# Extra matmuls of ten shapes ahead of 40 feed-forward outputs in each of two networks

## The reference, cut to what matters

```
first:  h = rms_norm(x);  u = conv3(h @ w_up);  gate, val = split(u)
        f = (gelu(gate) * val) @ w_down;  x = x + rms_norm(f)
second: hn = rms_norm(h);  out = h + (silu(hn @ w_gate) * (hn @ w_up)) @ w_down
```

## Time and profile before

| | |
|---|---|
| median of 2 runs | 870.45 us (870.25 to 870.66) |
| profiled execution | 873.64 us, of which 871.9 us from first to last instruction |
| granted TensorE clock, mean | 0.994 of 2.4 GHz |
| PE busy, PEld busy | 95%, 91% of the span |
| DVE, ACT, POOL busy | 73%, 57%, 36% |
| chain that ended last | PE 78%, DVE 10%, ACT 6%, issue 4% |
| DMA | 136 MB, engines busy 49% |

### The profile page before, as it was taken

How to read it: one execution, slowest core, us unless ns; L and a number is a source line. 1 busy time by engine, 2 the same in 40 slices (tenths; PEclk the granted TensorE clock), 3 DMA queues, 4 the chain that set the end, 5 groups by cost and what they waited for, 6 DMA issues and landing times.

```text
span 871.9 us, 16984 instructions
## 1 busy us (share of the span) xinstructions
PE 826.1 (95%) x6722; PEld 789.6 (91%) x6722; DVE 638.7 (73%) x981; ACT 498.8 (57%) x914; POOL 317.6 (36%) x148
## 2 busy tenths in 40 slices
PE   4999999999999999999999789899999999999998
PEld 3998889899999999788999779788999999999998
DVE  6895764888887772768799889955665676667774
ACT  6665655854665657756766474367546544444441
POOL 3843213122333225344466534332454223322321
PEclk9999999999999999999999999999999999999999
DMA  5743234355766665352656542322464457666651
GB/s 209 269 157 107 73 98 145 99 181 152 242 222 188 199 192 170 111 172 98 202 171 192 178 137 74 96 73 77 142 190 149 146 171 230 183 193 191 194 170 49
DMA packets 57246, 137.18 MB, mean 157 GB/s; under 512 B 6352, under 2 KB 27088, under 8 KB 57168
## 3 DMA queue, kind: packets, MB, share of 16 engines
q1 hardware_dynamic: 57168, 136.11, 49.4%
HBM read 135.03 MB, written 1.05 MB: 156 GB/s over the span
## 4 chain that ended last, share of the span: by engine, by line
PE 78%; DVE 10%; ACT 6%; issue 4%; DMA 1%; SPq 0%; DVEq 0%; ACTq 0%
PE PROD L626 15%; PE PROD L627 15%; PE PROD L628 15%; PE PROD L688 3%; PE OP L626 2%; PE OP L627 2%; PE OP L628 2%; PE SC L627 2%; PE TP L627 2%; PE TP L628 2%; PE SC L628 2%; PE TP L626 2%; PE SC L626 2%; DVE RS L1644 2%; PE OP L828 2%
## 5 line engine op out<-in xcount | busy, mean ns | idle before, releaser
L609 POOL TENSOR_TENSOR wlo<-raw,whi 128x1024 fp32r<-128x1024 f32 x124 | 314.0, 2538 | 533.8 <-ACT whi L1118 509.0
L626 PE MATMUL PROD<-HA,whi 128*128 128x256 f32 x1088 | 308.0, 283 | 13.1 <-DVE HA L1665 6.4
L627 PE MATMUL PROD<-HA,wlo 128*128 128x256 f32 x1088 | 302.9, 278 | 0.0
L628 PE MATMUL PROD<-HA,whi 128*128 128x256 f32 x1088 | 302.7, 278 | 0.0
L1118 ACT ACTIVATE whi<-raw 128x1024 fp32r<-128x1024 f32 x252 | 262.7, 1055 | 57.7 <-PE PROD L628 31.5
L1636 DVE TENSOR_TENSOR wlo<-raw,whi 128x1024 fp32r<-128x1024 f32 x128 | 191.0, 1495 | 82.4 <-ACT whi L1118 82.2
L626 PEld LDWEIGHTS PROD<-HA,whi 128*128 128x128 f32 x1088 | 205.9, 189 | 16.5 <-DVE HA L1665 7.0
L627 PEld LDWEIGHTS PROD<-HA,wlo 128*128 128x128 f32 x1088 | 205.3, 189 | 0.8 <-issue 0.7
L628 PEld LDWEIGHTS PROD<-HA,whi 128*128 128x128 f32 x1088 | 205.2, 189 | 0.0
L1644 DVE RECIPROCAL RS<-RTT 128x256 f32<-128x256 f32 (+2 forms) x18 | 42.8, 2380 | 16.6 <-ACT RTT L1137 16.5
L626 PE MATMUL OP<-HA,whi 128*128 128x256 f32 x192 | 53.7, 280 | 0.7 <-DVE KS L1721 0.5
(11 more groups left out here) (330 smaller groups left out, 1622.0 us busy)
## 6 DMA issues: line engine op xcount, KB each, us to landing
raw<-stream SPq DMA_DIRECT2D x197, 512.0 KB, 4.1
raw<-stream SPq DMA_DIRECT2D x144, 128.0 KB, 2.6
raw<-stream SPq DMA_DIRECT2D x28, 256.0 KB, 3.0
raw<-stream SPq DMA_DIRECT2D x4, 384.0 KB, 3.2
X<-xT SPq DMA_DIRECT2D x2, 512.0 KB, 5.5
out<-X SPq DMA_DIRECT2D x8, 128.0 KB, 2.0
KMEM<-memT SPq DMA_DIRECT2D x1, 512.0 KB, 5.4
VMEM<-memT SPq DMA_DIRECT2D x1, 512.0 KB, 6.1
```

The lines of the kernel that those rows point to most:

```text
L609: nc.gpsimd.tensor_tensor(wlo[:, n % NSPLIT, :], raw[:, n % NRAW, :], whi[:, n % NSPLIT, :].bitcast(F32), ALU.subtract).then_inc(lo_pool, 1)
L626: nc.tensor.matmul(dst, wh, hi, start=start, stop=False, skip_group_check=True)
L627: nc.tensor.matmul(dst, wl, hi, start=False, stop=False, skip_group_check=True)
L628: last = nc.tensor.matmul(dst, wh, lo, start=False, stop=stop, skip_group_check=True)
```

## The change

A list of ten shapes (stationary columns, moving columns, how often) is added, and `fm` uses it for the outputs 3 to 42 of "up" and "up2". Ahead of the 24 matmuls of such an output come one or more extra ones. They load the first `columns` columns of the output's first high block and stream the first `width` columns of the first chunk of `HA`'s high part past them, into the bank of the output. Each starts and ends its sum by itself, and the next one, and at last the output's own first matmul, overwrites it: no result of theirs is used. Each entry of the list serves four outputs in a row; the second of the four takes 128 by 128, once, in its place. The entry (P, P, 2) does two. The wait for the tile's low part is placed ahead of the extras as well as ahead of the first block.

```diff
+UNEVEN = [(P, 64, 1), (P, 192, 1), (P, 32, 1), (P, 224, 1), (64, S, 1), (P, 160, 1), (P, 96, 1), (P, P, 2),
+          (32, P, 1), (64, P, 1)]
 ...
                 k = KC[stage]
                 dst = begin((stage, m))[:, 0:S]
+                if stage in ("up", "up2") and 3 <= m < 3 + 4 * len(UNEVEN):
+                    n, i = divmod(POS[FIRST[stage] + m * k], BPT)
+                    if i == 0:
+                        split_wait(pe, n)
+                    columns, width, times = UNEVEN[(m - 3) // 4] if (m - 3) % 4 != 1 else (P, P, 1)
+                    for _ in range(times):
+                        nc.tensor.matmul(dst[0:columns, 0:width], whi[:, n % NSPLIT, i * P:i * P + columns],
+                                         H[:, base, 0:width], start=True, stop=True, skip_group_check=True)
                 for c in range(k):
```

## The result

The changed kernel took 889.44 us in the median of 2 runs (888.35 to 890.53), against 870.45 us before (870.25 to 870.66): a ratio of 1.0218 with a 95% interval of 1.0163 to 1.0273. That is 19.0 us more, 2.2%, where 890.4 us was forecast. The trace says why, and it also says that the forecast reached this number with one of its terms too large.

The account below looks back on a forecast made before the run. TensorE's matmul issue was taken to bound both networks; 9.7 us of slots, 0.8 of settling and 9.5 of slow pace made 20.0 us, so 893.6 from the profiled execution and 890.4 us from the median, range 879.8 to 895.5.

Parts of the forecast that it names:

- What bounds it: In both networks TensorE's issue of matmuls sets the time; added work there lengthens the kernel one to one.
- Term 1, the slots: Each of the 86 extras in the networks takes a wide matmul's slot of 0.1133 us, whatever its width: 9.7 us.
- the 3.1 us kept for them: Possible hiccup at the eighteen extras with 64 or 32 stationary columns, 0.17 us each; taken as 0 in the forecast.
- Term 2, the settling: At each of the 80 places the pace needs an estimated 0.01 us to settle: 0.8 us, bounds 0 and 1.6.
- Term 3, the pace: Wide matmuls behind extras in the networks partly fall to 0.1178 us a step: 9.5 us, bounds 0 and 13.6.
- the share of 0.7: Assumed part of the networks' 3024 wide matmuls running at the slow pace, giving 9.5 us.
- Sum: Slots, settling and slow pace in the networks together: 9.7 + 0.8 + 9.5 = 20.0 us.
- the 1.5 us either way that was allowed: Stages between the networks draw their paces anew: 0 in the sum, an estimated 1.5 us either way.
- the fast pace throughout: Rival: networks stay at 0.1133 us a step, so about 10 to 10.5 us more, 881 us; chance 0.22.
- All slow: Rival: every place in the networks ends slow, 24.1 us more, 894.6 us; no separate chance given.
- by columns: Rival: extras in the networks cost by their moving columns, loads hidden: 5.2 us, 875.7 us; chance 0.03.
- nothing at all: Rival: the extras vanish in idle time of PE, so the change does nothing; chance under 1 in 100.

Follow-up runs that it names:

- e3: One extra 128 by 128 matmul at output 3 of each network, two in all, against the kernel before: ratio 1.0157 (1.0101 to 1.0213).
- e4: Two extra 128 by 128 matmuls in a row at output 3 of each network, four in all, against the kernel before: ratio 1.0003 (0.9967 to 1.0040).
- the repeat: The changed kernel run once more unchanged, with the same 86 extras, against the kernel before: ratio 1.0197 (1.0148 to 1.0246).
- e5: One extra of 192 moving columns at each of the 80 places, against the kernel before: ratio 1.0065 (1.0028 to 1.0101).

## Why the prediction was right, point by point

- *What bounds it:* right. PE has no idle time in either network after, the chain is PE alone, and the added time stays. No other engine took over.
- *Term 1, the slots:* right, 0.1133 us for an extra whatever its columns. From the start of a single extra to that of the second wide matmul behind it the trace after has 0.226 to 0.236 us for every shape, and two slots are 0.227. 80 extras of 256 and 80 of 192 both cost 9.07 us. The eighteen with 64 or 32 stationary columns carry no price of their own; the 3.1 us kept for them were not needed. By the gap formula of the Trainium skill (TensorE: Matmul & The Clock Gate, "Back-to-back issue gap") the 192s would be cheaper than the 256s, an estimated 2.1 us over 80: the measurement decides against that here, where a load of 128 columns stands ahead of each matmul. But that section of the Trainium skill gives the formula for an isolated matmul, and says that in a stream of loads and matmuls both set the spacing; the prediction used it without this limit.
- *Term 2, the settling:* 0.8 us forecast, 0.5 measured.
- *Term 3, the pace:* the mechanism was right, the size was not. Two paces, settled at a disturbance and kept: e3 and e4 show it with two and four matmuls. But the share of 0.7 was 0.42 (1272 of 3036): 5.7 us in place of 9.5. I had taken the share as if each place were a draw. They are not: a short extra turns a fast network slow, and a later one, mostly the 128 by 128, turns it back (23 of 23), where the prediction had the slow pace as hard to leave. With 160 columns alone, where the 160 less often turns it back, the share was 0.70 (2112 of 3036).
- *Sum:* 20.0 us forecast; the networks gave 15.9. Outside them the change in pace is within the 1.5 us either way that was allowed: 1302 slow steps after against 1551 before, an estimated 1.1 us less. The profiled executions differ by 14.7 us (873.64 and 888.35). The first two runs of each kernel differ by 19.0 us (14.2 to 23.8), the runs of the repeat by 17.2 (13.0 to 21.5): both intervals take in 15.9, so nothing above it is shown to come from the change. The closeness of 890.4 to 889.44 is therefore in part luck: the sum was some 4 us too large, and it started from two runs at 870.45 us, below the medians of 873.9 to 875.6 us that the kernel before had beside the experiments.
- *Rivals:* the fast pace throughout (22 in 100) is what extras of 192 columns would have given. All slow (e3 shows what that takes), by columns, and nothing at all fell as above.

What sets the pace inside TensorE is open. A phase between loads and matmuls is the obvious idea, and the one form of it that I put to the test failed at three and five shorts.

## What to carry to other kernels

Where one engine is busy throughout, read its pace from starts before pricing a change there: a change of 4% in the step of 1500 instructions outweighs the instructions that are added. Keep the forms in a dense run of matmuls alike. In this kernel a piece left over was better issued at 192 columns or more, or as two; elsewhere that is to be tried, and the trace shows within a few steps which pace follows. And compare such kernels in the stage that changed: the whole time of this one scatters by more than many changes are worth.

## What was not expected of the hardware

Wide float32r matmuls (128x128 by 256) follow each other by 0.1133 or by 0.1178 us at the same granted clock of 1.00, for 1500 matmuls on end, and a single short matmul (32, 64, 128 or 160 moving columns) turned the first into the second in 54 of 54 places; 192 columns and more never did, in 13 of 13 and in all 80 places of e5. From the slow pace one 128 by 128 turned it back in 23 of 23. Two matmuls so placed cost 13.7 us, four cost 0.5.
